# Attention pipeline of a two-block transformer kernel: value products three units behind their scores, and a second buffer for the regrouped weights

## Chip, core and metric

The program runs on one core of one Trainium2 chip. The metric is the time of one execution in microseconds (us), of which the runs of the kernel before gave a median of 2311.57. Each execution computes the whole output for one sequence of 512 positions and 1024 features.

## What is computed

Two transformer blocks follow each other, in float32. The change touches the first, which has two layers. Each layer does this:

```python
h = rmsnorm(x, norm_g[layer])
u = einsum('bsd,dc->bsc', h, w_in[layer])          # all projections
ya = forgetting_attention(qa, ka, va, log_f)        # 4 heads, causal over 512 keys
yb = dilated_mixture_attention(rope(qb), rope(kb), vb)   # 6 heads
yc, _ = banded_attention(rope(qc), rope(kc), vc, 127, sinks[layer])  # 6 query heads, 2 key heads
merged = (sigmoid(ga) * (ya * silu(za)) @ w_br_a
          + sigmoid(gb) * (yb * silu(zb)) @ w_br_b
          + sigmoid(gc) * (yc * silu(zc)) @ w_br_c)
x = x + merged @ w_out[layer]
```

The second block (differential attention, convolution, cross attention, MLPs) has the same code in both kernels.

## The kernel before

**Matrix products.** A projection is computed a tile of 128 features by 512 positions at a time. Every float32 operand is split into a high and a low part in fp32r, so each of the 8 steps over the 1024 input features is three matmuls (lines 378 to 380). Three such matmuls are called a triple here. When a tile is done, VectorE evacuates it from PSUM; for tiles of q and k with rotary positions that is two SCALAR_TENSOR_TENSOR (L184), for the next weights one TENSOR_TENSOR of 1024 columns (L181, the low part of a weight tile), and later one addition (L178) of a half that four small DMAs have swapped between partitions (L825). The weights of values use a form with positions as rows (lines 404 to 406); two of its steps count as one triple.

**Attention.** The attention of a layer has three phases, named `forget`, `mix` and `sink`, with 6, 9 and 6 units. A unit is a pair of heads and one or two blocks of 128 queries. For each unit, in order:

1. *scores*: TensorE computes them (L581); VectorE adds bias and takes the maximum (a chain of L184, L178, L600, L187 in `forget`, L603 in the others), ScalarE takes the exponential (L190).
2. *norm*: VectorE takes the reciprocal (L624) and scales the weights into a buffer (L187).
3. *send*: SyncE issues a DMA of that buffer to DRAM (L664, `far<-t_Tb`).
4. *gather*: once it has landed, four DMAs bring it back in regrouped order (L672, `t_PTX<-far`) into the one tile of `grouped`.
5. *turn*: VectorE transposes blocks of 32 by 32 (L686, `t_PTb<-t_PTX`) into the one tile of `turned`.
6. *values*: TensorE multiplies with v (L726).

**What sets the order.** Each engine has one queue that it works through in the order of the program. `attention` is a generator with two yields for each unit; `drive` resumes another generator, the fill, a number of triples for each yield (`num/den`). The fill of `forget` is `gens_B`: 88 triples of projections, a gate tile, six rotary tiles of q and k, and the values. With 90/16 each yield brings 5.625 triples. In round i the loop issues values of unit i-2, scores of unit i, a yield, turn of unit i-1, norm and send of unit i, a second yield, and then the gather of unit i. The evacuation of a fill tile is issued when the triple after it is resumed, so at triples 9, 17, 25, 33 and so on.

Of the kernel before, what the change touches and what calls it, by code (L numbers as in the profile page):

```python
# [142 lines left out]
def lay_out(nc, A, plan, T):  # L143
# [196 lines left out]
    def drain():  # L340
        while late:
            flush()
# [76 lines left out]
    def drive(main, fill, num, den, lead=0):  # L419

        acc = 0
        for _ in range(lead):
            next(fill)
        for _ in main:
            acc += num
            while acc >= den:
                acc -= den
                if next(fill, 0) == 0:
                    acc = 0
                    break  # L430
        for _ in fill:
            pass
# [134 lines left out]
    def attention(units, done_pair, late_values=False, by_dma=False):  # L567
# [113 lines left out]
        def turn_near(u):  # L681

            n = 2 * (u["cols"] // 128)
            src, landed = u["near"]
            dst, dfree = turned.take()
            o = op(DV, lambda e: e.transpose(dst[:, 0:128 * n].rearrange("p (k i b) -> p k i b", i=4, b=32),  # L686
                                             src[:, 0:128 * n].rearrange("p (i k b) -> p k i b", i=4, b=32)),
                   landed, dfree)
            grouped.give(src, o)
            u["PT"] = [o]  # L690
            u["cut"] = [lambda k, h=h: dst[:, u["cols"] * h + k:u["cols"] * h + k + 128] for h in range(2)]
            u["held"] = dst
# [19 lines left out]
        def values(u):  # L712
            if u["first"]:
                st["O"] = [OB.take() for _ in range(u["nout"])]
            held = st["O"]
            if by_dma:
                cut, ready = u["cut"], u["PT"]
            else:
                cut = [lambda k, pt=pt: pt[:, k:k + 128] for pt, _ in u["PT"]]
                ready = [a for _, a in u["PT"]]  # L720

            def f(e):
                for k, (o, n, q) in enumerate(u["parts"]):
                    for j in range(n // 128):
                        for b, base, rows, vs, m in u["outs"]:
                            i = e.matmul(held[b][0][base:base + rows, 128 * q:128 * q + 128], vs[k][j],  # L726
                                         cut[m](o + 128 * j),
                                         start=j == 0, stop=j == n // 128 - 1)
                return i

            p = op(PE, f, ready, u["vtok"], *[x[1] for x in held] if u["first"] else [])
            if by_dma:
                turned.give(u["held"], p)
            else:
                for pt, _ in u["PT"]:
                    PTS.give(pt, p)
            if u["last"]:
                banks = [x[0] for x in held]
                frees = done_pair(u, banks, p)
                for b in banks:  # L740
                    OB.give(b, frees)
# [1 line left out]
        st["clear"] = op(DV, lambda e: e.memset(T["ST"][:, :, 8:16], 1.0), [f for _, f in STT.idle if f])  # L743
        n = len(units)
        if by_dma:
            for i in range(n + 2):
                if i >= 2:
                    values(units[i - 2])
                if i < n:
                    scores(units[i])  # L750
                yield
                flush()
                if 1 <= i <= n:
                    turn_near(units[i - 1])
                if i < n:
                    norm(units[i])
                    send_away(units[i])
                yield
                flush()
            return  # L760
# [164 lines left out]
    def gate_y(slots, zslots, ztok):  # L925
        def done(u, banks, p):
            i = u["pair"]
            t, free = TMP.take()
            o = op(DV, stt(t, banks[0], 0.5, Z[:, zslots[i], :], ALU.mult, ALU.mult), p, ztok[zslots[i]], free)
            split_into(YT, slots[i], t, o, give=t)  # L930
            return [o]
        return done
# [24 lines left out]
    for l in range(2):  # L957
# [95 lines left out]
        def gens_B(tok):  # L1053
            yield from gemm_fm(P0, WI(l, ZA + 128), parts8(), to_silu(1, ztok))
            for i in range(3):
                yield from gemm_fm(P0, WI(l, QB + 128 * i), parts8(), to_rope(0.125, qB[:, i, :], tok, ("q", i)))
            for i in range(3):
                yield from gemm_fm(P0, WI(l, KB + 128 * i), parts8(), to_rope(1.0, kB[:, i, :], tok, ("k", i)))
            yield from gemm_tm(P0, pair("w_in", l, VB), to_values([vB[:, :, 0:128], vB[:, :, 128:256]], tok,
                                                                  [("v", 0), ("v", 1)]))  # L1060
            yield from gemm_tm(P0, pair("w_in", l, VB + 256, VC),
                               to_values([vB[:, :, 256:384], vC[:, :, :]], tok, [("v", 2), ("vc", 0)]))

        def gens_C(tok):
            for i in range(3):
                yield from gemm_fm(P0, WI(l, ZB + 128 * i), parts8(), to_silu(2 + i, ztok))
            for i in range(3):
                yield from gemm_fm(P0, WI(l, QC + 64 * i, QC + 64 * (i + 3)), parts8(),
                                   to_rope(0.125, qC[:, i, :], tok, ("q", i)))
            yield from gemm_fm(P0, WI(l, KC), parts8(), to_rope(1.0, kC[:, 0, :], tok, ("k", 0)))  # L1070
            tok[("v", 0)] = tokB[("vc", 0)]
            yield from branch(l, GA, 2, [0, 1], "w_br_a", halves(0, 2), into_M(True))
# [6 lines left out]
        def units(kind, tok, npair, q, k, v):  # L1079
            out = []  # L1080
            groups = ((0, 1), (2, 3)) if kind == "sink" else ((0, 1), (2,), (3,))
            for pr in range(npair):
                for group in groups:
                    kt = 0 if kind == "sink" else pr
                    vc = 0 if kind == "sink" else 128 * pr
                    k0 = [max(0, 128 * (i - 1)) if kind == "sink" else 0 for i in group]
                    parts, at = [], 0
                    for i, s0 in zip(group, k0):
                        parts.append((at, 128 * (i + 1) - s0, i))
                        at += 128 * (i + 1) - s0  # L1090
                    u = dict(kind=kind, parts=parts, cols=at, pair=pr, nout=1, first=group[0] == 0,
                             last=group[-1] == 3, qk=[tok[("q", pr)], tok[("k", kt)]],
                             mm=[[(q[b:b + 64, pr, 128 * i:128 * i + 128], k[b:b + 64, kt, s0:s0 + n])
                                  for (_, n, i), s0 in zip(parts, k0)] for b in (0, 64)],
                             vtok=tok[("v", kt)],
                             outs=[(0, b, 64, [[v[:, s0 // 128 + j, vc + b:vc + b + 64] for j in range(n // 128)]
                                               for (_, n, _), s0 in zip(parts, k0)], b // 64) for b in (0, 64)])
                    if kind == "forget":
                        hh = (2 * pr, 2 * pr + 1)
                        u.update(cq=[[fg[:, 4, 4 * i + h:4 * i + h + 1] for i in group] for h in hh],  # L1100
                                 bias=[CB[:, h, :] for h in hh],
                                 diag=T["MC"][:, 128:256], btok=[ftok[hh[0]], ftok[hh[1]], ftok["cq"], c_MC])
                    elif kind == "sink":
                        u.update(bias=[T["MC"][:, 256 - n:256] for _, n, _ in parts], btok=[c_MC, c_sv],
                                 sink=[sv[:, SINK + 6 * l + h:SINK + 6 * l + h + 1] for h in (pr, pr + 3)])
                    else:
                        u.update(bias=[T["LC"][:, 512 - n:512] for _, n, _ in parts], btok=c_LC)
                    out.append(u)
            return out
# [6 lines left out]
            G.idle = [x for x in G.idle if x[0] is not spare[0] and x[0] is not spare[1]]  # L1116
            assert len(G.idle) == 3
        tokB, tokC = {}, {}
        drive(attention(units("forget", tok, 2, qA, kA, vA), gate_y([0, 1], [0, 1], ztok), by_dma=True), gens_B(tokB), 90, 16)
        drain()  # L1120
        drive(attention(units("mix", tokB, 3, qB, kB, vB), gate_y([2, 3, 4], [2, 3, 4], ztok), by_dma=True), gens_C(tokC), 138, 22)
        drain()
        drive(attention(units("sink", tokC, 3, qC, kC, vC), gate_y([5, 0, 1], [0, 1, 2], ztok), by_dma=True), gens_D(), 112, 16)
        drain()
        crow = [(64 * i, 64 * (i + 3)) for i in range(3)]
        run(branch(l, GC, 3, [5, 0, 1], "w_br_c", crow, into_P1))
        flush()
# [868 lines left out]
```

How the kernel before makes its waits and increments, by code:

```python
    def dma(self, eng, fn, sem, val, *deps):  # L94
        self.op(eng, lambda e: fn(e).then_inc(sem, 16), *deps)
        return Landed(sem, val)
# [9 lines left out]
    def play(self, eng, e):  # L106
        seen = {}
        for o in self.of[eng]:
            need = {}
            for d in o.deps:
                v = need.get(id(d.sem), (0, None))[0]
                need[id(d.sem)] = (max(v, d.val), d.sem)
            for k, (v, s) in need.items():
                if seen.get(k, 0) < v:
                    e.wait_ge(s, v)
                    seen[k] = v
            ins = o.fn(e)
            if o.sig:
                ins.then_inc(o.sem, 1)
# [23 lines left out]
def lay_out(nc, A, plan, T):  # L143
# [1646 lines left out]
                o = send(0, *((0, 3), (3, 3), (6, 2))[m - 3])  # L1790
                if m == 5:
                    SB.give(end[0]["row"][0], o)
    mlp(1, n2)
    drain()
    last_norm(1)
    last_row(1)
    for m, n in ((0, 3), (3, 3), (6, 2)):
        send(1, m, n)
    op(SP, lambda e: e.wait_ge(T["s_o"], 16 * sent[0]))
    return Q, used
```

## Time and profile before

| | |
|---|---|
| median of 3 runs | 2311.57 us (2308.72 to 2315.15) |
| profiled execution: its own time | 2313.52 us |
| its span, first to last instruction | 2311.7 us |
| TensorE busy | 2276.1 us, 98% of the span |
| VectorE busy | 1328.0 us, 57% |
| ScalarE busy | 817.5 us, 35% |
| HBM read and written | 227.64 and 22.03 MB |

A page of the profile gives busy time by engine over the whole span; the timeline gives each instruction with its start and length, and in brackets how long its engine was idle before it and on what. The name in brackets is inferred: an instruction that comes right behind the true one on the same engine may be named in its place.

### The profile page before, as it was taken

What the parts mean: (1) busy time and instruction counts of PE and PEld (TensorE: products, weight loads), DVE (VectorE), ACT (ScalarE), POOL (GpSimd) and SP (SyncE); (2) the same over time, 40 slices, a digit from 0 to 9 for tenths busy, and PEclk for the clock granted to TensorE, in tenths of its full rate; (3) what the DMA queues carried; (4) which work ended last, traced back from release to release, by engine and by line L of the source; (5) the groups of instructions that cost most, each with busy time, mean ns of one, the idle gap of its engine ahead of it and who ended that gap; (6) DMA issues with size and microseconds to landing.
All of it is one profiled execution on the core that took longest, in us unless ns stands there. A gap on an engine that the chain in (4) does not pass through costs nothing.

```text
span 2311.7 us, 28214 instructions
## 1 busy us (share of the span) xinstructions
PE 2276.1 (98%) x11210; PEld 1853.7 (80%) x11210; DVE 1328.0 (57%) x2259; ACT 817.5 (35%) x1335; POOL 13.9 (1%) x14
## 2 busy tenths in 40 slices
PE   9999999998999999999999999999999999999998
PEld 7677778877777787878898888888888888888887
DVE  5857675557667656576545544444755546444445
ACT  5323333432334334254333432332322334332233
POOL 0000000000000000200000000000000000000000
PEclk9999999999999999999999999999999999999999
DMA  5545442325454333323223222222222212223221
GB/s 175 155 133 172 150 139 96 109 87 170 144 167 146 117 98 113 120 74 131 88 86 134 91 96 96 91 100 92 91 101 92 91 46 97 95 92 100 91 97 59
DMA packets 113639, 255.45 MB, mean 111 GB/s; under 512 B 11839, under 2 KB 57535, under 8 KB 113380
## 3 DMA queue, kind: packets, MB, share of 16 engines
q1 hardware_dynamic: 113508, 253.64, 33.5%
q8 instruction: 89, 1.46, 0.3%
q14 instruction: 42, 0.34, 0.0%
HBM read 227.64 MB, written 22.03 MB: 108 GB/s over the span
## 4 chain that ended last, share of the span: by engine, by line
PE 90%; DVE 5%; DMA 2%; ACT 1%; SPq 1%; issue 0%; POOL 0%; POOLq 0%; DVEq 0%; ACTq 0%
PE ps L378 26%; PE ps L380 26%; PE ps L379 26%; PE ps L726 2%; PE ps L581 2%; DMA far<-t_Tb 1%; PE ps L404 1%; PE ps L405 1%; PE ps L1544 1%; PE ps L1494 1%; PE ps L406 1%; DMA t_PTX<-far 1%; DVE t_wlo L181 1%; PE ps L470 1%; DVE t_Tb L187 1%; DVE t_PTb L686 1%
## 5 line engine op out<-in xcount | busy, mean ns | idle before, releaser
L378 PE MATMUL ps<-t_P0H,t_whi 128*128 128x512 f32 x1664 | 669.0, 402 | 2.3 <-DVE t_P0L L184 2.3
L380 PE MATMUL ps<-t_P0H,t_wlo 128*128 128x512 f32 x1664 | 656.3, 394 | 0.0
L379 PE MATMUL ps<-t_P0L,t_whi 128*128 128x512 f32 x1664 | 655.6, 394 | 0.0
L190 ACT ACTIVATE t_whi<-t_raw 128x1024 fp32r<-128x1024 f32 (+3 forms) x395 | 404.6, 1028 | 429.5 <-PE ps L380 355.2
L181 DVE TENSOR_TENSOR t_wlo<-t_raw,t_whi 128x1024 fp32r<-128x1024 f32 (+3 forms) x394 | 468.2, 1189 | 49.1 <-PE ps L406 33.2
L378 PEld LDWEIGHTS ps<-t_P0H,t_whi 128*128 128x128 f32 x1664 | 313.7, 189 | 96.0 <-issue 23.3
L380 PEld LDWEIGHTS ps<-t_P0H,t_wlo 128*128 128x128 f32 x1664 | 313.2, 188 | 73.0
L379 PEld LDWEIGHTS ps<-t_P0L,t_whi 128*128 128x128 f32 x1664 | 313.5, 188 | 71.3 <-issue 2.4
L378 PE MATMUL ps<-t_P1H,t_whi 128*128 128x512 f32 (+1 forms) x932 | 361.2, 388 | 0.3 <-DVE t_P1L L181 0.3
L379 PE MATMUL ps<-t_P1L,t_whi 128*128 128x512 f32 (+1 forms) x932 | 359.5, 386 | 0.0
L380 PE MATMUL ps<-t_P1H,t_wlo 128*128 128x512 f32 (+1 forms) x916 | 355.5, 388 | 0.0
L378 PEld LDWEIGHTS ps<-t_P1H,t_whi 128*128 128x128 f32 x932 | 175.5, 188 | 38.7 <-DVE t_P1L L181 1.0
L379 PEld LDWEIGHTS ps<-t_P1L,t_whi 128*128 128x128 f32 x932 | 175.3, 188 | 37.4
L380 PEld LDWEIGHTS ps<-t_P1H,t_wlo 128*128 128x128 f32 x916 | 172.1, 188 | 37.9
L178 DVE TENSOR_TENSOR t_X<-ps,t_X 128x512 f32<-128x512 f32 (+1 forms) x136 | 89.7, 660 | 159.4 <-PE ps L380 159.4
L190 ACT ACTIVATE t_TMP<-t_TMP 128x512 f32<-128x512 f32 x92 | 58.2, 633 | 311.1 <-DVE t_TMP L184 229.3
L184 DVE SCALAR_TENSOR_TENSOR t_TMP<-ps,t_RB 128x512 f32<-128x512 f32 x64 | 44.3, 691 | 178.4 <-PE ps L380 178.3
L190 ACT ACTIVATE t_Tb<-t_Tb,t_ST 128x128 f32<-128x128 f32 (+3 forms) x96 | 51.6, 537 | 152.1 <-DVE t_ST L187 152.1
L184 DVE SCALAR_TENSOR_TENSOR t_X<-ps,t_X 128x512 f32<-128x512 f32 x48 | 33.2, 691 | 100.3 <-PE ps L380 100.3
L190 ACT ACTIVATE t_P0H<-t_X,t_gv 128x512 fp32r<-128x512 f32 x56 | 40.4, 725 | 138.1 <-DVE t_X L184 124.4
L190 ACT ACTIVATE t_P1H<-t_TMP 128x512 fp32r<-128x512 f32 x84 | 53.1, 633 | 84.6 <-DVE t_TMP L175 47.7
L181 DVE TENSOR_TENSOR t_P1L<-t_TMP,t_P1H 128x512 fp32r<-128x512 f32 x84 | 58.1, 691 | 23.0 <-ACT t_P1H L190 23.0
(239 smaller groups left out, 2359.3 us busy)
## 6 DMA issues: line engine op xcount, KB each, us to landing
t_raw<-in_wts SPq DMA_DIRECT2D x362, 512.0 KB, 3.5
far<-t_Tb SPq DMA_DIRECT2D x26, 384.0 KB, 2.9
t_PTX<-far SPq DMA_DIRECT2D x104, 96.0 KB, 2.1
far<-t_Tb SPq DMA_DIRECT2D x16, 512.0 KB, 3.3
t_PTX<-far SPq DMA_DIRECT2D x64, 128.0 KB, 2.6
t_raw<-in_wts SPq DMA_DIRECT2D x16, 384.0 KB, 3.0
t_raw<-in_wts SPq DMA_DIRECT2D x13, 256.0 KB, 2.7
t_raw<-in_wts SPq DMA_DIRECT2D x4, 520.0 KB, 5.3
```

Source lines behind the costliest of these rows:

```text
L178: return lambda e: e.tensor_tensor(o, a, b, ALU.add)
L181: return lambda e: e.tensor_tensor(o, a, b, ALU.subtract)
L184: return lambda e: e.scalar_tensor_tensor(out=o, in0=a, scalar=s, in1=b, op0=f, op1=g)
L187: return lambda e: e.tensor_scalar(o, a, s1, s2, f, g)
L190: return lambda e: e.activation(o, a, f, **k)
L378: e.matmul(bank[:, 0:N], wh, xh, start=first, stop=False)
L379: e.matmul(bank[:, 0:N], wh, xl, start=False, stop=False)
L380: return e.matmul(bank[:, 0:N], wl, xh, start=False, stop=end)
L404: e.matmul(out, xh, wh, start=k == 0, stop=False)
L405: e.matmul(out, xh, wl, start=False, stop=False)
L581: i = e.matmul(bank[:, o:o + n], l, r, start=True, stop=True)
L726: i = e.matmul(held[b][0][base:base + rows, 128 * q:128 * q + 128], vs[k][j], cut[m](o + 128 * j), start=j == 0, stop=j == n // 128 - 1)
```

## The change

The lag of values behind scores grows from two units to three, and the turn of a unit moves one round later with it, so that in every phase the loop has one round more. Two units' gathered weights are then held at once, so `grouped` gets a second tile in each phase: slots of `M` or `QKV` that hold nothing live then. The ratio of fill to yields is changed to 90/18, 138/24 and 112/18, so that the fill spreads over the two yields more.

```diff
@@ -743,15 +743,15 @@
         n = len(units)
         if by_dma:
-            for i in range(n + 2):
-                if i >= 2:
-                    values(units[i - 2])
+            for i in range(n + 3):
+                if i >= 3:
+                    values(units[i - 3])
                 if i < n:
                     scores(units[i])
                 yield
                 flush()
-                if 1 <= i <= n:
-                    turn_near(units[i - 1])
+                if 2 <= i <= n + 1:
+                    turn_near(units[i - 2])
                 if i < n:
                     norm(units[i])
                     send_away(units[i])
@@ -1116,12 +1116,18 @@
-        drive(attention(units("forget", tok, 2, qA, kA, vA), gate_y([0, 1], [0, 1], ztok), by_dma=True), gens_B(tokB), 90, 16)
-        drain()
-        drive(attention(units("mix", tokB, 3, qB, kB, vB), gate_y([2, 3, 4], [2, 3, 4], ztok), by_dma=True), gens_C(tokC), 138, 22)
-        drain()
-        drive(attention(units("sink", tokC, 3, qC, kC, vC), gate_y([5, 0, 1], [0, 1, 2], ztok), by_dma=True), gens_D(), 112, 16)
-        drain()
+
+        def phase(kind, tk, npair, q, k, v, slots, zslots, fill, num, den, more):
+
+            grouped.idle.append((wide(more), None))
+            drive(attention(units(kind, tk, npair, q, k, v), gate_y(slots, zslots, ztok), by_dma=True), fill, num, den)
+            grouped.idle = [x for x in grouped.idle if x[0].tensor.name == T["PTX"][:, :, :].tensor.name]
+            assert len(grouped.idle) == 1
+            drain()
+
+        phase("forget", tok, 2, qA, kA, vA, [0, 1], [0, 1], gens_B(tokB), 90, 18, M[:, 4:6, :])
+        phase("mix", tokB, 3, qB, kB, vB, [2, 3, 4], [2, 3, 4], gens_C(tokC), 138, 24, QKV[:, 4:6, :])
+        phase("sink", tokC, 3, qC, kC, vC, [5, 0, 1], [0, 1, 2], gens_D(), 112, 18, QKV[:, 6:8, :])
```

**TensorE, third scores of the `forget` phase in layer 0.** Before, 22 triples have gone by, and the first values (L726) stand ahead of the third scores (L581):

```order
L380 MATMUL ps<-t_P0H,t_wlo 128x512
L726 MATMUL ps<-t_PTb,t_QKV 64x128 x6
L581 MATMUL ps<-t_QKV 128x512 x2
L378 MATMUL ps<-t_P0H,t_whi 128x512
L379 MATMUL ps<-t_P0L,t_whi 128x512
```

Now the third scores come after 20 triples, with no values ahead of them:

```order
L380 MATMUL ps<-t_P0H,t_wlo 128x512
L581 MATMUL ps<-t_QKV 128x512 x2
L378 MATMUL ps<-t_P0H,t_whi 128x512
L379 MATMUL ps<-t_P0L,t_whi 128x512
L380 MATMUL ps<-t_P0H,t_wlo 128x512
```

The first values have moved to the round after, behind 30 triples, ahead of the four blocks of the fourth scores.

**VectorE, behind the score chain of the second unit in the same phase.** The piece of the difference:

```order
 L600 TENSOR_REDUCE t_ST<-t_TbX 128x1
 L187 TENSOR_SCALAR t_ST<-t_ST 128x1
-L686 STREAM_TRANSPOSE t_PTb<-t_PTX 128x768
 L624 RECIPROCAL t_ST<-t_ST 128x4
 L187 TENSOR_SCALAR t_Tb<-t_Tb,t_ST 128x3x4x32
```

The first turn has left this place. It now stands behind the score chain of the third unit and the evacuation of a rotary tile. There the queue of the changed kernel reads:

```order
L187 TENSOR_SCALAR t_ST<-t_ST 128x1
L184 SCALAR_TENSOR_TENSOR t_TMX<-ps,t_sinT 128x512
L184 SCALAR_TENSOR_TENSOR t_QKV<-ps,t_cosT 128x512
L181 TENSOR_TENSOR t_wlo<-t_raw,t_whi 128x1024
L178 TENSOR_TENSOR t_QKV<-t_QKV,t_TMX 128x512
L686 STREAM_TRANSPOSE t_PTb<-t_PTX 128x768
```

In the kernel before the same six rows stand there too, but the turn at their end is that of the second unit.

## Rows read from the trace of the kernel before

**Rows 1.** The page, part 1: busy time of the engines.

```profile
PE 2276.1 (98%) x11210; PEld 1853.7 (80%) x11210; DVE 1328.0 (57%) x2259; ACT 817.5 (35%) x1335; POOL 13.9 (1%) x14
```

**Rows 2.** Waits of TensorE, matmul and weight load, 60 to 780 us: total, times, longest.

```profile
PE ps L726 <- DVE t_ST L624: 11.3, 7, 2.7
PE ps L726 <- DVE t_PTb L686: 7.6, 2, 4.5
...
PEld ps L378 <- issue: 20.5, 49, 0.8
```

**Rows 3.** Windows over the `forget` phases of layers 0 and 1: length, busy, clock, DMA.

```profile
54.96:142.84 87.88, 78.33 (x474) 63.64 (x473) 63.60 (x128) 24.06 (x48) 0.00 (x0) 0.94 0.46 138
...
497.37:582.86 85.49, 75.99 (x474) 62.01 (x473) 63.43 (x128) 24.07 (x48) 0.00 (x0) 0.98 0.46 142
```

**Rows 4.** Timeline of TensorE, `forget` phases: start, length, line, tiles, idle before.

```profile
63.67 0.92 PE L581 MATMUL ps<-t_QKV 64*128 64x384 f32 x4
...
73.19 0.88 PE L726 MATMUL ps<-t_PTb,t_QKV 128*64 128x128 f32 x12 [0.79 <-DVE t_ST L624]
74.00 1.13 PE L581 MATMUL ps<-t_QKV 64*128 64x512 f32 x4
...
85.76 1.25 PE L726 MATMUL ps<-t_PTb,t_QKV 128*64 128x128 f32 x12 [2.72 <-DVE t_ST L624]
...
108.68 0.88 PE L726 MATMUL ps<-t_PTb,t_QKV 128*64 128x128 f32 x12 [1.36 <-DVE t_ST L624]
...
132.22 1.97 PE L726 MATMUL ps<-t_PTb,t_QKV 128*64 128x128 f32 x16 [4.49 <-DVE t_PTb L686]
...
573.03 1.09 PE L726 MATMUL ps<-t_PTb,t_QKV 128*64 128x128 f32 x16 [3.14 <-DVE t_PTb L686]
```

**Rows 5.** Windows at the stretches of lower clock; the clock follows the counts.

```profile
86.00:90.00 4.00, 4.00 (x24) 2.75 (x21) 4.00 (x8) 0.00 (x0) 0.00 (x0) 0.57 0.77 262
130.00:138.00 8.00, 5.78 (x36) 5.46 (x37) 3.38 (x5) 0.63 (x1) 0.00 (x0) 0.57 0.20 83
574.00:578.00 4.00, 4.00 (x24) 3.95 (x21) 2.14 (x4) 0.63 (x1) 0.00 (x0) 0.57 0.00 0
```

**Rows 6.** Timeline of VectorE, 66 to 85 us, layer 0.

```profile
66.79 0.61 DVE L184 SCALAR_TENSOR_TENSOR t_Tb<-ps,t_fg,t_M 128x384 f32<-128x384 f32 x1
...
69.98 0.15 DVE L187 TENSOR_SCALAR t_ST<-t_ST 128x1 f32<-128x1 f32 x1
...
72.16 0.98 DVE L686 STREAM_TRANSPOSE t_PTb<-t_PTX 128x768 f32<-128x768 f32 x1 [2.03 <-DMA t_PTX<-far]
73.06 0.14 DVE L624 RECIPROCAL t_ST<-t_ST 128x4 f32<-128x4 f32 x1
...
74.36 0.68 DVE L175 TENSOR_TENSOR t_cosT<-t_cosT,t_RB 128x512 f32<-128x512 f32 x1
...
78.01 0.75 DVE L184 SCALAR_TENSOR_TENSOR t_Tb<-ps,t_fg,t_M 128x512 f32<-128x512 f32 x1
...
81.80 0.68 DVE L184 SCALAR_TENSOR_TENSOR t_TMX<-ps,t_sinT 128x512 f32<-128x512 f32 x1
...
84.73 0.97 DVE L686 STREAM_TRANSPOSE t_PTb<-t_PTX 128x768 f32<-128x768 f32 x1
```

**Rows 7.** Timeline of ScalarE: the last exponential of the second unit, layer 0.

```profile
70.69 0.19 ACT L190 ACTIVATION_READ_ACCUMULATOR t_TbX<-t_TbX,t_ST 128x1 f32 x1
```

**Rows 8.** Timeline of VectorE: the last turn of the phase.

```profile
130.92 1.25 DVE L686 STREAM_TRANSPOSE t_PTb<-t_PTX 128x1024 f32<-128x1024 f32 x1 [4.57 <-DMA t_PTX<-far]
```

**Rows 9.** Timeline of the `mix` phase, layer 0: a turn and its values.

```profile
201.78 0.97 DVE L686 STREAM_TRANSPOSE t_PTb<-t_PTX 128x768 f32<-128x768 f32 x1
...
205.00 0.88 PE L726 MATMUL ps<-t_PTb,t_QKV 128*64 128x128 f32 x12
```

**Rows 10.** Timeline of TensorE: two successive first matmuls of triples at full clock.

```profile
150.01 0.40 PE L378 MATMUL ps<-t_P0H,t_whi 128*128 128x512 f32 x1
...
150.70 0.40 PE L378 MATMUL ps<-t_P0H,t_whi 128*128 128x512 f32 x1
```

## Prediction

> **What bounds the kernel.** I read the page first: TensorE is busy 98% of the span [rows 1], so a change of order that adds and removes no work can only touch what is left, and the question is where TensorE waits. The waits of TensorE between 60 and 780 us, which is where the attention of the first block lies, come to 11.3 + 7.6 = 18.9 us, all ahead of values (L726) [rows 2]. The timeline puts every one of them in a `forget` phase: in layer 0 they are 0.79, 2.72, 1.36 and 4.49 us, together 9.36 [rows 4], which leaves 18.9 - 9.36 = 9.5 us for layer 1. Each wait can cost more than itself, because the granted clock then falls to the 1.2 GHz level for a while. A mean of 0.57 over 4 us means 0.43 x 4 = 1.7 us of work lost; that happened after the 2.72 us wait and after the last wait of layer 1. Around the 4.49 us wait the clock was low from 130 us on; TensorE was at work for 5.78 of those 8 us, and over the 5.8 us at work the loss is about 2.5 [rows 5].
>
> So the `forget` phase holds 9.36 + 1.7 + 2.5 = 13.6 us of loss in layer 0 and 9.5 + 1.7 = 11.2 in layer 1. The windows agree: 87.88 - 13.6 = 74.3 and 85.49 - 11.2 = 74.3 us [rows 3]. Two phases with the same instructions have the same floor. At most 24.8 us are to be had. The phases `mix` and `sink` show no wait on VectorE.
>
> **What kind of wait they are.** This decides the forecast, for the change attacks a transfer. Two kinds are to be told apart in VectorE's timeline. At the end of the phase the last turn is itself idle for 4.57 us on the gather [rows 8]: a late transfer. So is the first turn, idle 2.03 us. But the turn at 84.73, on which the 2.72 us wait hangs, has no idle time ahead of it: from 72.16 to 85.70 VectorE works without a break (norm, rotary tables, a tile, the score chain, a tile, an addition) [rows 6]. Its gather had landed. The wait is for VectorE's queue, and only the 2.03 us idle at its head comes from a DMA.
>
> **The change, end of the phase.** The last unit is sent after yield 11, gathered after yield 12, turned after yield 15 and used after yield 16; before, turned after 13 and used after 14. At 5 triples a yield, and 0.69 us a triple [rows 10], gather and turn are now 15 triples or 10.4 us apart instead of one yield of 3.9 us, and the turn was 4.57 us short. It has 1.9 us over. Its values come after 80 of the 88 triples, so work remains behind them. The last waits go: 4.49 + 2.5 = 7.0 us in layer 0. In layer 1 it is 3.14 [rows 4] + 1.7 = 4.8.
>
> **The change, start of the phase.** I replay VectorE's queue in the new order with lengths from the same rows (start to next start). Scores of unit 1 come one triple earlier on TensorE, 63.67 - 0.69 = 62.98 [rows 4], but VectorE reaches them at 66.79 in either order, because it is already behind. The chain ends at 70.13. There is no turn to wait for; norm waits only for the exponential, 70.88 [rows 7], and takes 1.3, to 72.2. Then tables and a tile 3.65 (74.36 to 78.01), the chain of unit 2 3.79 (to 81.80), a tile and an addition 2.93 (to 84.73): 82.6 [rows 6]. Then the first turn, after whose start values could begin 1.03 us later (85.76 - 84.73): **83.65**. TensorE meanwhile: scores 1.11 more than its triples (73.19 - 0.79 - 63.67 - 11 x 0.693), ten triples 6.93, scores of 512 columns 1.42 (85.76 - 2.72 - 74.00 - 7.62), ten triples 6.93: 62.98 + 16.4 = **79.4**. The first values wait 4.3 us in each layer. The reason in one sentence: between the second scores and the first values VectorE has 16.9 us of work and TensorE 16.4, VectorE starts 3.8 us late, and the 2.03 us that it no longer idles don't pay for that, because ten triples a round instead of 11.25 take 0.87 us a round from the cover.
>
> Such a wait drew a low clock twice in rows of like length: loss 1.7 to 2.5, taken as 2.1. Then VectorE turns over norm (about 1.04), the chain of four blocks (its elements are fewer, its instructions more; taken as 3.9, like that of unit 2), an addition and a tile (2.9) and the turn (1.03), with scores answered some 1.1 us after their start: values of unit 1 are ready about 94.3; TensorE arrives at 83.65 + 0.81 + 1.15 + 6.93 + 2.1 = 94.6. No wait (0.9 without the low clock). By the same steps unit 2 waits 0.6 (its turn has 1024 columns, 1.3) and unit 3 waits 0.7, for a gate evacuation stands ahead of its scores. Units 4 and 5 wait for nothing: all score chains are over. Sum per layer: 4.3 + 2.1 + 0 + 0.6 + 0.7 = 7.7 us. The bounds per layer: 6.0 if the clock holds and the late ones vanish; 10.5 if each of three later waits is 1.5.
>
> **The change, one stop more.** Every phase has one round more, so one pair of values and scores that stood side by side is split. Returning to the triples costs TensorE's weight load 0.42 us (20.5/49) [rows 2], part of it under the draining matmul. I take 0.3, bounds 0 and 0.42: six phases, 1.8 us.
>
> **The change, rest.** The second tile costs no instruction; sends, gathers and turns are as many as before, in the same queues. SyncE still waits for a send to land ahead of its gather, with weights queued behind, as before. In `mix` and `sink` the half round shrinks by 0.52 and 0.78 triples, 0.36 and 0.54 us. The closest turn that I found there ended 205.00 - 202.75 = 2.25 us ahead of its values [rows 9], so it stays covered; if it isn't, each of the 30 units pays.
>
> **Sum.** Layer 0: 13.6 - 7.7 = 5.9 won; layer 1: 11.2 - 7.7 = 3.5; less 1.8: **7.6 us**. The profiled execution's own time is 2313.52, so 2305.9 by it; the median of the runs shown lies 1.95 lower, so I forecast **2304**. About 0.3% (6.9 us) is what a measurement of this kernel can tell from no change, and this lies at that line.
>
> **Rivals.**
> - *The transfer was the cause of all the waits.* Then all 24.8 go, less 1.8: 23 us, 2288.5. For it speaks that the chain of the first wait begins with 2.03 us on a DMA; against it, the turn at 84.73 with no idle ahead. The Trainium skill (Trainium Kernel Development and Optimization, Best Practices) says "Double-buffer for performance: Overlap DMA with compute"; the page by itself would have this rival, and the trace agrees for the last turn of the phase alone. 8%.
> - *VectorE catches up more than I allow.* The first wait is 2.9 us, with no low clock and nothing later: 13.6 + 11.2 - 5.8 - 1.8 = 17.2 won, 2294.5. It needs VectorE to enter the second chain 1.4 us sooner; but in both layers the row order ahead of it is unchanged. 12%.
> - *Nothing on balance.* Later waits of 1.5 us each and the low clock at its dearer end: 10.5 to 12 us a layer, so 24.8 - 21 to 24 - 1.8, 2 us or less won: 2309 to 2314. For it: VectorE is busy 63.6 of 87.9 us [rows 3], and nearly all in its first two thirds. 14%.
> - *Slower.* The queue of VectorE is never emptied while score chains last, and each of the four values of units 0 to 3 waits over 2.7 us and draws a low clock: 4 x (3 + 1.7) = 18.8 us a layer, 37.6 against 24.8, + 1.8: 14.6 lost, 2326. It decides once a layer loses over 11.5 us. Against it: a low clock delays TensorE by itself, so VectorE regains the time. 8%.
> - The worked case: 58%, own range 2299 to 2309.
>
> **Chances.** Of the worked case 34 lie over 0.3% and 24 within. Faster 0.34 + 0.08 + 0.12 = 0.54; same 0.24 + 0.14 = 0.38; slower 0.08. The range 2296 to 2311 leaves out the first rival, the last, and a part of the second.
>
> **What the profile would show.** Right: no idle of L686 on a DMA in any phase; no wait and full clock at the end of both `forget` phases; one wait of 3.5 to 5 us ahead of the first values in each layer, near 83 us, with VectorE working without a break ahead of it, and a low clock behind it; two waits of under 1.5 us after; `forget` phases of 82.3 us each (74.3 + 7.7 + 0.3); `mix` and `sink` phases 0.3 us longer. Wrong: if the first values wait under 2.5 us, my replay of VectorE's queue has failed; if waits appear in `mix` or `sink`, the cover there was misjudged.

## The result, and the profile after

The change made the kernel slower. The median of 6 runs is 2319.52 us (2319.36 to 2321.83), against 2310.57 (2308.72 to 2315.15) of 6 runs of the kernel before: a ratio of 1.0038, interval 1.0025 to 1.0051. The forecast was 2304, its range ended at 2311. The profiled execution took 2319.36 us; its span is 2317.6, or 5.9 more than before.

The page of the changed kernel, part 1, shows the same work as [rows 1]: the same instruction counts on every engine, TensorE 2.3 us longer.

```profile
PE 2278.4 (98%) x11210; PEld 1853.1 (80%) x11210; DVE 1327.4 (57%) x2259; ACT 817.3 (35%) x1335; POOL 13.9 (1%) x14
```

TensorE's waits around the attention of the first block, the first two lines of that view: the answer to [rows 2].

```profile
PE ps L726 <- DVE t_ST L624: 11.6, 7, 4.5
PE ps L726 <- DVE t_PTb L686: 10.9, 2, 6.1
```

They were 11.3 + 7.6 = 18.9 us and are 22.5. The forecast has only the first line, at about 4.3 + 0.6 + 0.7 a layer. The second, two waits of which the longest is 6.1 us, should not be there. Windows over the two `forget` phases (length; busy time of TensorE, its weight load, VectorE, ScalarE and GpSimd; clock; share and rate of the DMAs), then over stretches with a low clock, and over the `mix` phase of layer 0:

```profile
54.07:144.03 89.96, 77.90 (x473) 63.11 (x472) 63.45 (x128) 24.17 (x48) 0.00 (x0) 0.94 0.47 135
144.03:257.38 113.35, 113.23 (x577) 85.43 (x576) 78.16 (x170) 41.24 (x82) 0.00 (x0) 1.00 0.52 158
499.34:588.19 88.85, 78.47 (x473) 63.56 (x472) 63.44 (x128) 24.18 (x48) 0.00 (x0) 0.94 0.45 137
83.00:87.00 4.00, 4.00 (x24) 2.74 (x21) 2.05 (x6) 0.00 (x0) 0.00 (x0) 0.57 0.91 280
124.00:131.00 7.00, 3.84 (x23) 3.51 (x24) 1.58 (x2) 0.00 (x0) 0.00 (x0) 0.51 0.30 94
571.00:575.00 4.00, 3.31 (x21) 2.98 (x22) 0.64 (x1) 0.00 (x0) 0.00 (x0) 0.57 0.17 68
```

The phases took 87.88 and 85.49 us [rows 3] and take 89.96 and 88.85, where 82.3 was forecast. That is 2.1 + 3.4 = 5.4 us. `mix` has grown from 112.84 to 113.35 in both layers, and the stretch from there to the next layer from 241.69 to 241.96; behind the `mix` phase of layer 1 the difference is 0.06. That is 5.4 + 2 x 0.51 + 0.27 + 0.06 = 6.8 us. The stretch ahead of the first `forget` phase, which the change doesn't touch, is 0.9 shorter (54.07 against 54.96, at a clock of 1.00 against 0.97), which leaves the 5.9. The medians differ by more, 9.0 us; how the waits of before vary from one execution to the next is seen in an experiment below.

The timeline of TensorE shows the five values (L726) of the `forget` phase in layer 0 that had to wait; the sixth, at 137.16 us, had no idle time ahead. It answers to [rows 4].

```profile
82.75 1.18 PE L726 MATMUL ps<-t_PTb,t_QKV 128*64 128x128 f32 x12 [4.38 <-DVE t_ST L624]
93.50 0.88 PE L726 MATMUL ps<-t_PTb,t_QKV 128*64 128x128 f32 x12 [0.34 <-DVE t_ST L624]
102.82 1.09 PE L726 MATMUL ps<-t_PTb,t_QKV 128*64 128x128 f32 x16 [0.41 <-DVE t_ST L624]
112.92 0.88 PE L726 MATMUL ps<-t_PTb,t_QKV 128*64 128x128 f32 x12 [0.78 <-DVE t_ST L624]
127.16 1.55 PE L726 MATMUL ps<-t_PTb,t_QKV 128*64 128x128 f32 x12 [6.15 <-DVE t_PTb L686]
```

Four waits are those of the forecast. The fifth, ahead of the values of unit 4 (units are counted from 0), is new: 6.15 us here, and in layer 1 it is 4.73. After it the clock is at the 1.2 GHz level: 0.51 over 7 us, in which TensorE worked 3.84 us, so some 1.8 us lost. Sum for layer 0: waits 12.1, low clock 1.7 (0.43 x 4 us) + 1.8, and 74.3 + 15.6 = 89.9. In layer 1 the low clock costs 0.43 x 3.31 = 1.4 us after the fifth wait, and more than in layer 0 after the first:

```profile
528.00:532.00 4.00, 3.90 (x22) 2.82 (x23) 1.64 (x6) 0.00 (x0) 0.00 (x0) 0.50 0.85 266
532.00:534.00 2.00, 2.00 (x6) 1.58 (x6) 1.90 (x7) 0.57 (x3) 0.00 (x0) 0.56 0.08 28
```

That is 0.50 x 3.90 + 0.44 x 2.00 = 2.8 us. Sum for layer 1: waits 10.4, low clock 2.8 + 1.4, and 74.3 + 14.6 = 88.9.

What is the turn of unit 4 waiting for? VectorE's timeline just ahead of it:

```profile
116.60 1.22 DVE L181 TENSOR_TENSOR t_wlo<-t_raw,t_whi 128x1024 fp32r<-128x1024 f32 x1
117.74 0.75 DVE L175 TENSOR_TENSOR t_QKV<-ps,t_RC 128x256 f32<-128x256 f32 x2
125.52 0.69 DVE L178 TENSOR_TENSOR t_QKV<-t_QKV,t_TMP 128x512 f32<-128x512 f32 x1 [7.04 <-DMA t_TMP<-t_TMX]
126.13 0.97 DVE L686 STREAM_TRANSPOSE t_PTb<-t_PTX 128x768 f32<-128x768 f32 x1
```

The turn has no idle time of its own; its data is there. The instruction ahead of it is idle for 7.04 us. It is the addition of the last rotary tile, and it waits for a swap (L825), a DMA that has nothing to do with attention. SyncE's queue says why. After:

```profile
114.07 0.40 SPq L664 DMA_DIRECT2D far<-t_Tb  x1
119.09 2.54 SPq L672 DMA_DIRECT2D t_M<-far  x4
121.67 2.42 SPq L825 DMA_DIRECT2D t_TMP<-t_TMX  x4
124.19 0.53 SPq L218 DMA_DIRECT2D t_raw<-in_wts  x1
```

The same place before:

```profile
114.16 1.76 SPq L672 DMA_DIRECT2D t_PTX<-far  x4
115.96 2.42 SPq L825 DMA_DIRECT2D t_TMP<-t_TMX  x4
118.48 0.53 SPq L218 DMA_DIRECT2D t_raw<-in_wts  x1
119.79 0.39 SPq L664 DMA_DIRECT2D far<-t_Tb  x1
125.42 1.74 SPq L672 DMA_DIRECT2D t_PTX<-far  x4
```

A gather may start only when its send has landed, and everything behind it in the queue waits with it. Before, the swap of the last rotary tile (115.96) stood ahead of the last send (119.79). Now the last send has gone first (114.07), its gather waits until 119.09 for it to land, and the swap, whose half tile VectorE had ready by about 116.1 (L184 at 115.41), is issued at 121.67.

### The profile page after: what moved, and what is told of

It reads as the page before. It is cut to its first block, busy times and chain, and to the rows that moved or that the text cites. A ratio compares the mean times of both kernels' runs of the same rounds, so it can differ in the third digit from the quotient of the medians.

```text
span 2317.6 us, 28222 instructions
## 1 busy us (share of the span) xinstructions
PE 2278.4 (98%) x11210; PEld 1853.1 (80%) x11210; DVE 1327.4 (57%) x2259; ACT 817.3 (35%) x1335; POOL 13.9 (1%) x14
## 4 chain that ended last, share of the span: by engine, by line
PE 91%; DVE 6%; ACT 1%; DMA 1%; issue 1%; POOL 0%; SPq 0%; POOLq 0%; DVEq 0%; ACTq 0%
PE ps L378 26%; PE ps L380 26%; PE ps L379 26%; PE ps L726 2%; PE ps L581 2%; PE ps L404 1%; PE ps L405 1%; PE ps L406 1%; PE ps L1550 1%; PE ps L1500 1%; DVE t_wlo L181 1%; PE ps L470 1%; DVE t_ST L600 1%; POOL t_UP L178 0%; DVE t_Tb L187 0%
## 5 line engine op out<-in xcount | busy, mean ns | idle before, releaser
L181 DVE TENSOR_TENSOR t_wlo<-t_raw,t_whi 128x1024 fp32r<-128x1024 f32 (+3 forms) x394 | 468.1, 1189 | 48.2 <-PE ps L406 32.4
L184 DVE SCALAR_TENSOR_TENSOR t_TMP<-ps,t_RB 128x512 f32<-128x512 f32 x64 | 44.3, 692 | 178.3 <-PE ps L380 178.3
L184 DVE SCALAR_TENSOR_TENSOR t_X<-ps,t_X 128x512 f32<-128x512 f32 x48 | 33.2, 691 | 100.3 <-PE ps L380 100.3
L181 DVE TENSOR_TENSOR t_P1L<-t_TMP,t_P1H 128x512 fp32r<-128x512 f32 x84 | 58.1, 691 | 24.1 <-ACT t_P1H L190 23.8
```

The source lines that it names most:

```text
L181: return lambda e: e.tensor_tensor(o, a, b, ALU.subtract)
L184: return lambda e: e.scalar_tensor_tensor(out=o, in0=a, scalar=s, in1=b, op0=f, op1=g)
```

## The experiments

Each ratio is against runs of the kernel before on the same chip, with its 95% interval. All edits are made to the changed kernel. The theory: the fifth wait is this order in SyncE's queue, and the other four are VectorE's own work. The rivals: the fifth wait is VectorE's load too; the loss is in `mix` and `sink`; the second tile costs by itself.

**The gather one flush later, so that the swap passes it.**

```diff
-            later(rest)
+            later(rest, 2)
```

> The changed kernel, with each gather issued one flush later, so that the swap of the last rotary tile stands ahead of the last gather in SyncE's queue. Theory (queue order: the swap waits behind a gather that waits for a send to land, VectorE's addition waits for the swap, the turn and the values wait for the addition): the 6.15 and 4.73 us waits ahead of the fifth values in the two forget phases go, with the low clock around them (about 1.8 us each), so 14 us less than the changed kernel: about 2305 us; the first wait of 4.4 us in each layer stays. Rival (the swap itself is slow because weights, send and gather share the DMA engines): the addition still waits over 4 us and the time stays near 2319.

Measured: 2304.06 us (2303.47 to 2304.71), ratio 0.9971 (0.9960 to 0.9983). The `forget` phases take 82.61 and 82.39 us. SyncE's queue, and below it one row of VectorE, one of TensorE and the window of the phase:

```profile
114.14 0.38 SPq L664 DMA_DIRECT2D far<-t_Tb  x1
115.30 2.41 SPq L825 DMA_DIRECT2D t_TMP<-t_TMX  x4
118.38 3.50 SPq L672 DMA_DIRECT2D t_M<-far  x4
```

```profile
119.15 0.69 DVE L178 TENSOR_TENSOR t_QKV<-t_QKV,t_TMP 128x512 f32<-128x512 f32 x1 [1.41 <-DMA t_TMP<-t_TMX]
...
82.30 1.55 PE L726 MATMUL ps<-t_PTb,t_QKV 128*64 128x128 f32 x12 [4.38 <-DVE t_ST L624]
...
53.62:136.23 82.61, 77.03 (x473) 62.38 (x473) 63.42 (x128) 24.18 (x48) 0.00 (x0) 0.96 0.51 147
```

The swap goes out 6.4 us earlier, the addition waits 1.41 us in place of 7.04, and the fifth wait is gone. The first stays at 4.38. One line takes back 15.5 us of the median. Of that the `forget` phases give 13.8 in the profiled executions (89.96 + 88.85 against 82.61 + 82.39). Most of the rest, 1.6 us, lies behind the `mix` phase of layer 1, a stretch that differs by 1.9 us between the profiles of the kernel before and of the one with the second tile alone.

**The swap issued by ScalarE.** The same question by another road: SyncE's order stays, only the swap leaves its queue.

```diff
-                swapped = Q.dma(SP, lambda e, s=s, d=d: e.dma_start(b[d:d + 32, :], u[s:s + 32, :]),
+                swapped = Q.dma(AC, lambda e, s=s, d=d: e.dma_start(b[d:d + 32, :], u[s:s + 32, :]),
```

> The changed kernel, gathers where they are, but the four swap DMAs of every rotary tile issued from ScalarE's queue in place of SyncE's. Theory (SyncE's queue holds the swap back until the send has landed): the swap of the last rotary tile is issued right behind its first evacuation, at about 117 us in layer 0, the 7 us idle of VectorE goes, and with it the 6.15 and 4.73 us waits: 2304 to 2308 us, as with the gather behind the swap. Rival (the DMA engines are loaded): the addition still waits over 4 us.

Measured: 2304.05 us (2303.06 to 2307.01), ratio 0.9966 (0.9956 to 0.9977). The swap now overtakes the waiting gather:

```profile
115.07 2.44 ACTq L825 DMA_DIRECT2D t_TMP<-t_TMX  x4
...
116.87 2.01 SPq L672 DMA_DIRECT2D t_M<-far  x4
```

No fifth wait; the others are 4.38, 0.41 and 0.80, the phases 81.83 and 82.06. Two different edits that share only this, that the swap no longer stands behind a waiting gather, give the same time. The Trainium skill (DMA: Bandwidth & Descriptors, "Issuing engines are not separate DMA queues") says that issuing on several engines only saves the sequencer's time to initiate. By that, the addition would be spared at most the swap's 2.42 us of issue. The trace shows more: the swap is issued 6.6 us earlier, and the addition is idle for 1.86 us in place of 7.04, since SyncE's sequencer was not issuing but waiting for the send. The wait for that send is itself shorter here, 2.9 us in place of 5.0, but the swap no longer depends on it.

**The old ratio of fill to yields.** 90/16, 138/22 and 112/16 again, with the lag of three kept; the lines of `mix` and `sink` change in the same way as the one shown.

```diff
-        phase("forget", tok, 2, qA, kA, vA, [0, 1], [0, 1], gens_B(tokB), 90, 18, M[:, 4:6, :])
+        phase("forget", tok, 2, qA, kA, vA, [0, 1], [0, 1], gens_B(tokB), 90, 16, M[:, 4:6, :])
```

> The changed kernel with the old ratios 90/16, 138/22 and 112/16, so that the third lag and the second buffer act without the fill being spread thinner; the last round of each phase then has no fill. Theory (the first wait is VectorE's queue against ten triples a round): with 11.25 triples TensorE arrives at the first values 2.1 us later, 81.4 against 83.65, so the first wait falls from 4.4 to about 2.2 us and draws no low clock; the swap of the last rotary tile is issued after triple 56 and the last send after 61, so the long fifth wait goes too. The last values come after 84 of 88 triples: still covered. Forget phases of about 78 us, in all about 2300 us. Rival (the lag of three itself costs, wherever the fill stands): near 2319.

Measured: 2300.87 us (2298.57 to 2303.47), ratio 0.9957 (0.9943 to 0.9971). Again no fifth wait: with more triples a yield, the last send comes after the last swap. The first wait of layer 1 (4.46 us in the changed kernel):

```profile
517.59 0.88 PE L726 MATMUL ps<-t_PTb,t_QKV 128*64 128x128 f32 x12 [2.35 <-DVE t_ST L624]
```

In layer 0 it is 2.27. The thinner fill of the change thus did both things: it took 2.1 us of cover from each first value, and it moved the last send ahead of the last swap. Not all waits are gone: in layer 1 the values of unit 2 wait 2.94 us (540.33), with a clock of 0.58 behind them, and the phases take 79.62 and 81.74 us where about 78 was expected; the time expected for the whole came out all the same. `mix` is back at 112.86. So the 0.5 us that it had grown wasn't for the extra round as such, which this kernel has too (the stretch behind it stays at 241.93); a likely reason, argued and not shown, is that the fill is used up by then, so that no triple stands between the parts.

**The second tile alone**, with lag 2 and the old ratios.

```diff
-            for i in range(n + 3):
-                if i >= 3:
-                    values(units[i - 3])
+            for i in range(n + 2):
+                if i >= 2:
+                    values(units[i - 2])
...
-                if 2 <= i <= n + 1:
-                    turn_near(units[i - 2])
+                if 1 <= i <= n:
+                    turn_near(units[i - 1])
```

> The kernel before with the second tile for gathered weights alone: lag two, old ratios. Theory: at a lag of two a gather is always issued behind the turn that frees the only tile, and that turn is long done, so the second tile changes nothing: within 2 us of the kernel before. Rival (gathers wait for the tile): the 4.49 and 3.14 us waits at the phase ends shrink and the kernel is 5 us or more faster.

Measured: 2311.04 us (2307.4 to 2317.6), ratio 1.0002 (0.9992 to 1.0012). Without the lag the buffer is worth nothing and costs nothing that the interval would show (2 to 3 us either way), so "Double-buffer for performance: Overlap DMA with compute", the rule of the Trainium skill (Trainium Kernel Development and Optimization, Best Practices) that made the first rival, gives nothing here by itself. The waits, in the profiled execution:

```profile
PE ps L726 <- DVE t_ST L624: 11.5, 7, 2.7
PE ps L726 <- DVE t_PTb L686: 4.6, 2, 2.7
```

The second line is 4.6 us here and was 7.6 in [rows 2], in an execution with the same order: the end-of-phase waits of the lag of two vary by some us between executions. The `forget` phases take 85.32 and 85.86 us here, together 2.2 less than in the profile of before. Two profiles of the same order can therefore differ by 2 us and more in these phases.

**The new lag in `mix` and `sink` only**; `forget` keeps lag 2 and 90/16.

```diff
+            g = 2 if units[0]["kind"] == "forget" else 3
-            for i in range(n + 3):
-                if i >= 3:
-                    values(units[i - 3])
+            for i in range(n + g):
+                if i >= g:
+                    values(units[i - g])
...
-                if 2 <= i <= n + 1:
-                    turn_near(units[i - 2])
+                if g - 1 <= i <= n + g - 2:
+                    turn_near(units[i - g + 1])
```

> The forget phases as in the kernel before (lag two, 90/16), mix and sink as in the changed kernel. Theory: nothing waits there on VectorE in either, and the round more costs one stop of TensorE in four phases, 0.3 to 0.5 us each: 1 to 2 us slower than the kernel before, which cannot be told from no change. Rival (mix and sink take part in the loss): 4 us or more slower.

Measured: 2314.03 us (2311.69 to 2317.79), ratio 1.0009 (1.0000 to 1.0018); `mix` takes 113.35 as in the changed kernel. By the medians the cost there is 1.9 us, and the interval leaves 0 to 4. It isn't where the forecast broke.

**A cheaper maximum in `forget`**: it is taken over every eighth column, so part of the computation is left out. This takes load off VectorE, ahead of the first values above all.

```diff
-                        s[:, c + k:c + k + 1], t[:, o:o + n], axis=AX), a) for k, (o, n, _) in enumerate(parts)]
+                        s[:, c + k:c + k + 1], t[:, o:o + n:8], axis=AX), a) for k, (o, n, _) in enumerate(parts)]
```

> The changed kernel with the maximum of each forget score row taken over every eighth column in place of all (part of the computation left out), which makes VectorE's reductions of 0.55 to 0.69 us short and touches nothing else. Theory (two causes: VectorE's amount of work sets the first waits, SyncE's order sets the fifth): by the first values VectorE has six long reductions less, about 3 us, so the first wait falls from 4.4 to 1 to 1.5 us and the later small ones go, about 4 us less wait and one low clock less in each layer; the fifth wait stays at 4 to 7 us with its low clock. In all about 2307 us. Rival (the fifth wait too is VectorE's load): it shrinks by as much as VectorE is ahead, and the time is under 2300 us.

Measured: 2317.09 us (2315.86 to 2318.85), ratio 1.0026 (1.0016 to 1.0035), some 10 us above what was expected. The first and the fifth wait of layer 1, and the addition ahead of the first turn of layer 0:

```profile
526.04 0.88 PE L726 MATMUL ps<-t_PTb,t_QKV 128*64 128x128 f32 x12 [2.42 <-DVE t_ST L624]
...
570.51 1.55 PE L726 MATMUL ps<-t_PTb,t_QKV 128*64 128x128 f32 x12 [8.36 <-DVE t_PTb L686]
...
81.29 0.69 DVE L178 TENSOR_TENSOR t_QKV<-t_QKV,t_TMX 128x512 f32<-128x512 f32 x1 [1.83 <-DMA t_TMX<-t_TMX]
```

With less work for VectorE the fifth wait grows, to 6.93 and 8.36 us: it isn't VectorE's load. Its turn starts when it did (125.81 and 569.48, against 126.13 and 570.67), and TensorE is there sooner. The first wait was expected at 1 to 1.5 us. It falls to 2.42 in layer 1, but stays at 4.29 in layer 0, because there the addition ahead of the turn now waits 1.83 us for a swap, issued at 77.37 behind the second gather (75.58). So in layer 0 the order in SyncE's queue is a second limit of the first wait, close behind VectorE's load.

**The turn earlier.** If the first wait is work queued ahead of the turn, moving the turn right behind the values, ahead of the scores, should remove it.

```diff
                 if i >= 3:
                     values(units[i - 3])
+                if 2 <= i <= n + 1:
+                    turn_near(units[i - 2])
                 if i < n:
                     scores(units[i])
                 yield
                 flush()
-                if 2 <= i <= n + 1:
-                    turn_near(units[i - 2])
```

> The changed kernel with each turn issued at the start of its round, right behind the values that free its tile and ahead of the score chain, a half round earlier on VectorE. Theory (every wait left is a turn standing behind a chain, a tile or an addition in VectorE's queue): the first turn can start at about 76 us, TensorE needs it at 79.4, so no value waits over 0.5 us, the low clocks of the forget phases go, and the fifth turn is ahead of the late addition. Forget phases of 74.6 to 76 us, in all 2288 to 2291 us. Rival (VectorE is the bound of the stretch, whatever its order): the waits move to evacuations or weights and the time is over 2300 us.

Measured: 2313.5 us (2312.27 to 2315.57), ratio 1.0015 (1.0006 to 1.0024). That is some 23 us more than expected. The first wait is gone, but now the values of unit 4 wait 4.45 us, and behind them a product of the projection of v (L404) waits for the low part of its weights (L181), which VectorE has behind an addition that waits 5.17 us for its swap:

```profile
119.30 1.55 PE L726 MATMUL ps<-t_PTb,t_QKV 128*64 128x128 f32 x12 [4.45 <-DVE t_PTb L686]
128.06 0.39 PE L404 MATMUL ps<-t_whi,t_P0H 128*128 128x256 f32 x1 [3.41 <-DVE t_wlo L181]
...
125.05 0.69 DVE L178 TENSOR_TENSOR t_QKV<-t_QKV,t_TMP 128x512 f32<-128x512 f32 x1 [5.17 <-DMA t_TMP<-t_TMX]
```

**The turn earlier and the gather one flush later**, with the changed ratio:

> The changed kernel with both edits: each turn at the start of its round, and each gather one flush later, behind the swap of the tile. Theory (two separate causes, each undone by its own edit: a turn that stands behind VectorE's own work, and an addition that stands behind a gather in SyncE's queue): neither the first wait nor the long waits in the second half of the forget phases are left, under 3 us of waits ahead of values in all, no low clock in the forget phases, about 2290 us. Rival (VectorE has too much work in the first 60 triples in any order): waits of 3 us or more move to other places of the forget phases, 2298 us or more.

Measured: 2311.9 us (2310.55 to 2314.88), ratio 1.0001 (0.9992 to 1.0011), again some 22 us more than expected. The last turn now comes so early that it idles on its own gather, and the weights' low part stands behind it:

```profile
123.55 1.25 DVE L686 STREAM_TRANSPOSE t_PTb<-t_M 128x1024 f32<-128x1024 f32 x1 [4.63 <-DMA t_M<-far]
...
125.96 0.58 PE L404 MATMUL ps<-t_whi,t_P0H 128*128 128x256 f32 x1 [5.70 <-DVE t_wlo L181]
```

**The same with the old ratio.**

> The same with the old ratios 90/16, 138/22 and 112/16. Theory: with both causes gone the ratio matters only through VectorE's load for each round, so the time is within 3 us of the kernel with the new ratios, about 2290 us. Rival (the thinner fill is what puts VectorE behind in any order): 5 us or more faster than the kernel with the new ratios.

Measured: 2297.17 us (2295.83 to 2298.41), ratio 0.9937 (0.9924 to 0.9949); the phases take 78.78 and 78.66, with no wait ahead of values, and 3.19 and 3.02 left at L404. The ratio alone is worth 14.7 us here, where the theory had under 3: its rival came true, the thinner fill puts VectorE behind in this order too.

**Early turns only while scores follow, swap on ScalarE.**

```diff
+                if 2 <= i < n:
+                    turn_near(units[i - 2])
                 if i < n:
                     scores(units[i])
                 yield
                 flush()
-                if 2 <= i <= n + 1:
+                if n <= i <= n + 1:
                     turn_near(units[i - 2])
```

> The changed kernel with swaps issued from ScalarE's queue, and turns at the start of the round only while score chains still follow; the last two turns stay in mid round, so that no weights stand behind a turn that waits for its gather. Theory (three queue positions explain all waits of the forget phase: a turn behind a score chain and a tile, an addition behind a gather, weights behind a turn): the first wait of 4.4 us, the long fifth wait and the weights' wait of 5 us are all gone; what is left is 1 to 2 us ahead of the fourth values. Forget phases of 75 to 77 us each, in all 2290 to 2294 us. Rival (VectorE is simply overloaded in the first 60 triples, so a wait removed in one place returns in another): forget phases of 80 us or more, 2300 us or more.

Measured: 2305.63 us (2304.97 to 2308.68), ratio 0.9977 (0.9967 to 0.9987), not the 2290 to 2294 hoped for. The first wait of 4.38 us is gone, and two others have come:

```profile
107.99 0.88 PE L726 MATMUL ps<-t_PTb,t_QKV 128*64 128x128 f32 x12 [1.17 <-DVE t_PTb L686]
...
118.86 0.69 DVE L178 TENSOR_TENSOR t_QKV<-t_QKV,t_TMP 128x512 f32<-128x512 f32 x1 [1.51 <-DMA t_TMP<-t_TMX]
...
120.50 0.89 PE L726 MATMUL ps<-t_PTb,t_QKV 128*64 128x128 f32 x12 [4.43 <-DVE t_PTb L686]
```

1.17 + 4.43 = 5.60; with the turns in their old place it was 4.38 + 0.41 + 0.80 = 5.59. In layer 1 it is 5.70 against 5.97, and the phases take 81.40 and 81.75 us against 81.83 and 82.06. That is the rival of this expectation: with this fill, the order seems only to decide at which values TensorE pays. It is argued from the sums and not shown, for part of the 4.43 us isn't VectorE's work: the addition ahead of that turn is idle for 1.51 us on its swap (1.87 in layer 1).

**The same with the old ratio.**

> The same with the old ratios 90/16, 138/22 and 112/16. Theory: 11.25 triples a round give VectorE 0.87 us more a round, the wait of 1 to 2 us ahead of the fourth values goes too, forget phases of 74.3 to 75.5 us, in all 2286 to 2290 us, the best of all kernels here. Rival (with the old ratios the last values come too near the end of the fill): the last values wait over 2 us and the kernel is no faster than with the new ratios.

Measured: 2300.75 us (2299.36 to 2301.16), ratio 0.9951 (0.9939 to 0.9964), against 2286 to 2290 expected. What is left is a wait of 4.40 and 4.45 us at L404, behind an addition that waits 2.61 and 2.67 us for its swap:

```profile
112.39 2.44 ACTq L827 DMA_DIRECT2D t_TMP<-t_TMX  x4
...
118.44 0.69 DVE L178 TENSOR_TENSOR t_QKV<-t_QKV,t_TMP 128x512 f32<-128x512 f32 x1 [2.61 <-DMA t_TMP<-t_TMX]
```

The swap isn't issued late. The half tile is ready at about 112.4 us (L184 at 111.68, 0.68 long), and in the next kernel, where SyncE issues the swap, it goes out at 112.34. It lands late: the slowest of its four DMAs takes 4.2 us, and 4.3 in layer 1, against 2.5 and 2.0 in the next kernel. Here SyncE is free to issue a load of weights beside the last of the four (114.12); there that load goes out behind them (115.05). That this load is what slows the swap is likely, and was not tried apart.

**The best version.** The same early turns and old ratios, the swap back on SyncE and the gather one flush later instead.

> Early turns while scores follow, gathers one flush later, swaps on SyncE as before, old ratios. Theory: in the kernel with all turns early the weights' low part stood behind the last turn, which waited for its gather, and TensorE waited 3.2 and 3.0 us with a low clock in each layer; with the last turn in mid round that wait goes: 2297 less about 9, near 2288 us. Rival (the late gather is then the bound): the last values wait 3 us or more and the time stays near 2297.

Measured: 2293.22 us (2292.1 to 2294.19), ratio 0.9919 (0.9904 to 0.9934). It beats both kernels, and is 5 us above what was expected.

```profile
53.94:131.83 77.89, 75.59 (x474) 61.91 (x473) 62.83 (x127) 24.35 (x48) 0.00 (x0) 0.98 0.56 156
...
118.25 0.58 PE L404 MATMUL ps<-t_whi,t_P0H 128*128 128x256 f32 x1 [2.29 <-DVE t_wlo L181]
```

The phases take 77.89 and 77.84 us, 3.6 above their floor of 74.3, of which 2.29 and 2.17 is the wait at L404.

## Why the prediction was wrong

*End of the phase.* Right in its step and outweighed by another. The last values wait for nothing, and the last turn doesn't idle on its gather.

*Start of the phase.* Right: 4.38 and 4.46 us for a forecast of 4.3, with VectorE at work without a break ahead of it and a low clock behind it, which cost 1.7 and 2.8 us for a forecast of 2.1. Both ends of the wait came out, in layer 0: 78.37 and 82.75 us for 79.4 and 83.65, in a phase that starts 0.9 earlier. The reason given, two rounds that are thinner in fill, is shown by the run with the old ratio: 2.1 us less wait. The sparse maximum bears out VectorE's load in layer 1; in layer 0 a swap then holds the values nearly as long (4.29 us). The later waits came as worked out: 0.34 and none (forecast 0), 0.41 and 0.40 (0.6), 0.78 and 0.79 (0.7).

*Units 4 and 5.* This is the step that failed: "Units 4 and 5 wait for nothing: all score chains are over." It asked only what score chains stand ahead of the turn on VectorE. The values of unit 4 wait 6.15 and 4.73 us, with 1.8 and some 1.4 us of low clock, 14.1 us over both layers. The sentence that came nearest says: "SyncE still waits for a send to land ahead of its gather, with weights queued behind, as before". That wait is as before, but what is queued behind it isn't. The send of the last unit had moved from after the last rotary tile to before it, and so the tile's swap came to stand behind the gather, the addition behind the swap, the turn of unit 4 behind the addition. With this one order mended, by either of two edits, the kernel takes 2304.06 and 2304.05 us, and its `forget` phases 82.61 and 82.39 with the first edit, 81.83 and 82.06 with the second, where the forecast has 82.3. The phases bear the rest of the forecast out; that the medians meet 2304 to a tenth is luck, for the runs of before beside them have medians of 2310.4 and 2312.14, and the forecast started from 2311.57.

*One stop more.* 1.8 us were forecast for six phases, 1.2 for the four of `mix` and `sink`. The windows give 1.4 for these four, and the run with the new lag in them alone 1.9, with an interval of 0 to 4. The size isn't contradicted; the reason (a return to the triples after each extra round) is doubtful, since `mix` is back at 112.86 us with the old ratio, extra round and all.

*The rivals.* That the transfer caused all waits is false: with the gather long landed, the first values still wait 4.38 and 4.46 us, behind a VectorE that works without a break. That VectorE catches up is false with this ratio. The slower rival's condition, over 11.5 us lost in a layer, was met (15.6 and 14.6). But it had the right sign by a wrong mechanism: not four waits over 2.7 us from VectorE's queue, but one from SyncE's on top of the forecast one.

*Left open.* The profiles differ by 5.9 us and the medians by 9.0. The executions of before spread over 6.4 us and those of after over 2.5, and the profiled one of before is itself 3 us above its median. The profile of the buffer alone, with the same order, has a span 4.8 us shorter: 0.7 of it ahead of the first `forget` phase, 2.2 in the two `forget` phases and 1.9 behind the `mix` phase of layer 1. Which of these make up the missing 3 us in a median run of before, no profile shows.

## What to carry to other kernels

When a change moves a DMA that waits for another to land, list everything that comes to stand behind it on the engine that issues it, also what belongs to other work, and follow each of these to who waits for it. Here it was the wait for the landing that cost, so a later place or another engine's queue was a cure. And where the engine that evacuates has as much queued for a round as TensorE, look at the fill that covers each round before its order: with the thin fill, once the swap was out of the gather's way, earlier turns gained nothing (2311.9 and 2305.63 us against 2304.06 and 2304.05); with the fuller fill, early turns and the later gather took the kernel from 2300.87 to 2293.22 us.

## What the runs showed of the hardware

A send of 512 KB took 5.0 us to land (114.07 to 119.09), against a median of 3.1 for the 16 sends of that size in the whole program. A load of weights had been issued 0.6 us ahead of it. In the kernels with the gather one flush later and with the swap on ScalarE, where no weights were issued in the 4 us ahead of the same send, it took 3.0 and 2.9 us in layer 0. That the weights make the difference fits these rows, and was not tried apart.

The low clock didn't follow the length of the wait alone: the 2.27 us wait of layer 0 with the old ratio was followed by values that took 1.48 us in place of 0.88, and the 2.35 us wait of layer 1 by values of 0.88, at full speed, with a clock of 0.57 over the 4 us from 83 us and of 1.00 over the 9 us from 517:

```profile
83.10 1.48 PE L726 MATMUL ps<-t_PTb,t_QKV 128*64 128x128 f32 x12 [2.27 <-DVE t_ST L624]
```
